# Two layers of a two-block transformer on one core: another order of steps in the first block's mixing stage

## What is computed

```
mod = silu(c) @ w_mod + b_mod;  h = rms(x, ln1) * (1 + sc1) + sh1
p = h @ w_in     # qa ka va | qi ki wi | qb kb vb | qc kc vc, heads of 64
x = x + g1 * (rms(concat(oa, ob, oc)) @ w_o)
h = rms(x, ln2) * (1 + sc2) + sh2
x = x + g2 * (silu(h @ w_gate) * (h @ w_up)) @ w_down
```

## Time and profile before

| | |
|---|---|
| median of 3 runs | 3133.84 us (3128.38 to 3138.25) |
| the profiled execution | 3130.37 us, its span 3128.6 us |
| PE busy | 2908.3 us (93%) |
| DVE busy | 1787.2 us (57%) |
| ACT busy | 756.2 us (24%) |
| POOL busy | 931.1 us (30%) |
| DMA | 313.28 MB, mean 100 GB/s |

### The profile page before, as it was taken

The page is one execution under the profiler, slowest core; times in us unless marked ns, Lnnn a source line. Parts: engine busy times, 40 slices in busy tenths (PEclk is TensorE's granted clock), DMA queues, the critical chain, the costliest instruction groups (busy, mean ns, idle before and its releaser), DMA issues.

```text
span 3128.6 us, 33693 instructions
## 1 busy us (share of the span) xinstructions
PE 2908.3 (93%) x12126; PEld 2133.1 (68%) x12126; DVE 1787.2 (57%) x3803; ACT 756.2 (24%) x1781; POOL 931.1 (30%) x794
## 2 busy tenths in 40 slices
PE   8888999999997899999989988999999998899997
PEld 4354688888544578888854456888884454688886
DVE  2673469388367447938854545877824634551433
ACT  2354310000235431000022353201112335320111
POOL 0301224443330124444412202344440400344442
PEclk9989999999998799999989988999999998899998
DMA  6115034244221013434421101254421210122221
GB/s 256 64 61 215 28 138 166 101 148 170 91 80 61 1 55 121 175 108 156 154 76 56 61 27 68 108 183 186 156 100 57 59 50 23 40 94 96 81 81 54
DMA packets 45412, 313.28 MB, mean 100 GB/s; under 512 B 5424, under 2 KB 5552, under 8 KB 31040
## 3 DMA queue, kind: packets, MB, share of 16 engines
q1 hardware_dynamic: 42912, 306.88, 27.0%
q10 hardware_dynamic: 2304, 4.20, 0.6%
q0 software_dynamic: 32, 0.07, 0.0%
HBM read 298.53 MB, written 2.10 MB: 96 GB/s over the span
## 4 chain that ended last, share of the span: by engine, by line
PE 70%; DVE 18%; ACT 6%; issue 3%; DMA 1%; POOL 1%; DVEq 0%; SPq 0%; ACTq 0%; POOLq 0%
PE bank L1114 39%; PE bank L1094 9%; PE bank L1440 7%; PE bank L1168 3%; DVE nw L2067 3%; PE bank L1264 2%; DVE sel L2304 2%; DVE m L2303 1%; PE bank L1307 1%; DVE SPT L2368 1%; ACT SPT L1756 1%; PE bank L1294 1%; PE bank L1229 1%; PE bank L1567 1%; DMA sel<-in_mod_pieces 1%
## 5 line engine op out<-in xcount | busy, mean ns | idle before, releaser
L1000 POOL TENSOR_TENSOR SPT<-ring 128x512 f32<-128x512 f32 (+2 forms) x140 | 175.2, 1252 | 956.3 <-DMA ring<-in_slabs 493.0
L1114 PE MATMUL bank<-U,ring 128*128 128x256 f32 x1728 | 412.2, 384 | 10.8 <-DVE U L2101 10.5
L1114 PEld LDWEIGHTS bank<-U,ring 128*128 128x128 f32 x1728 | 332.8, 193 | 58.4 <-DVE U L2101 12.5
L2067 DVE SCALAR_TENSOR_TENSOR nw<-sel,c,nw 128x256 f32<-128x256 f32 x504 | 321.7, 638 | 31.2 <-DMA sel<-in_mod_pieces 13.5
L1114 PE MATMUL bank<-U,SPT 128*128 128x256 f32 x1296 | 312.5, 381 | 3.0 <-POOL SPT L1005 3.0
L1114 PEld LDWEIGHTS bank<-U,SPT 128*128 128x128 f32 x1296 | 247.4, 191 | 37.7 <-POOL SPT L1005 4.4
L1114 PE MATMUL bank<-hT,SPT 128*128 128x256 f32 x1088 | 257.1, 379 | 0.0
L1440 PE MATMUL bank<-hT,ring 128*128 128x512 f32 x544 | 249.7, 607 | 7.1 <-ACT hT L1873 7.1
L2127 DVE TENSOR_TENSOR rb<-bank,nw 128x256 f32<-128x256 f32 x108 | 45.5, 422 | 355.9 <-PE bank L1114 259.1
L1114 PE MATMUL bank<-hT,ring 128*128 128x256 f32 x1088 | 246.1, 379 | 0.0
L1114 PEld LDWEIGHTS bank<-hT,ring 128*128 128x128 f32 x1088 | 207.0, 190 | 28.0 <-DMA ring<-in_slabs 0.3
(11 more groups left out here) (344 smaller groups left out, 4501.9 us busy)
## 6 DMA issues: line engine op xcount, KB each, us to landing
ring<-in_slabs SPq DMA_DIRECT2D x86, 2048.0 KB, 8.0
sel<-in_mod_pieces SPq DMA_DIRECT2D x144, 512.0 KB, 4.5
ring<-in_slabs SPq DMA_DIRECT2D x8, 1536.0 KB, 7.0
ring<-in_slabs SPq DMA_DIRECT2D x8, 1280.0 KB, 8.3
tab<-U SPq DMA_DIRECT2D x40, 128.0 KB, 2.0
U<-in_slabs SPq DMA_DIRECT2D x2, 2048.0 KB, 22.5
tmp<-nw ACTq DMA_DIRECT2D x16, 256.0 KB, 2.9
ring<-in_slabs SPq DMA_DIRECT2D x2, 1808.0 KB, 11.7
```

The lines of the kernel that those rows point to most:

```text
L1000: pool.tensor_tensor(e1, a21, a22, ALU.add).then_inc(*pool_order.up())
L1114: mm = pe.matmul(into[j][:, c:c + HALF], lhs[:, k, :], rhs[:, k, :], start=(begin and k == 0), stop=(end and k == kp - 1))
L2067: ins = dve.scalar_tensor_tensor(a, w[:, k, :], c[:, j:j + 1], a, ALU.mult, ALU.add)
```

## The change

1. The tiles are projected in the order 2, 0, 1, 10, ... instead of 0, 1, 2, 10, ... Since slabs hold four tiles in this order, the table of weights is cut by the same list.
2. The values of block 1 come first (`V_ORDER`), the rest one by one behind `idx 1`, `idx 2` and `idx 3`, each with three rounds of top-k. The weighted index sum waits only for its own block's values.
3. One weave takes the place of two: dense tiles over -0.01 to 0.48, all fourteen groups over 0.2 to 0.95, the other top-k rounds over 0 to 0.5, the stick-breaking heads over 0.5 to 0.96, the modulation products over 0.45 to 0.74 (layer 0), `wo 0` from 0.74 (layer 0) or 0.68 (layer 1) to 1.02.
4. Waits follow: the key exchange of the index tile is issued by SP one tile later, `idx` waits for the rope of tile 1, and the value consumers for the last of `V_ORDER`.

```diff
--- before.py
+++ after.py
@@ -177,12 +177,13 @@
 
 PROJ, ROWS, TURN, OUT, SMALL = (0, 1), (2, 3), (4, 5), (6,), (7,)
 QI, KI, KA, QA, QB, KB, KC, QC = 0, 2, 3, 4, 6, 8, 10, 12
-TILES1 = (0, 1, 2, 10, 12, 13, 14, 15, 4, 5, 6, 7, 8, 9)
+TILES1 = (2, 0, 1, 10, 12, 13, 14, 15, 4, 5, 6, 7, 8, 9)
+V_ORDER = (1, 2, 3, 0)
 NT1 = len(TILES1)
 ROPED = [n for n in TILES1 if n not in (6, 7, 8, 9)]
 NORMED = [n for n in ROPED if n > 1]
 SHARED = (KI, KC)
-TURNED_BEHIND = {("v", 0): ROPED[:2], ("kq", 0): ROPED[2:3], ("qa", 0): ROPED[3:6], ("qb", 0): ROPED[6:]}
+TURNED_BEHIND = {("v", 0): ROPED[:3], ("kq", 0): ROPED[3:4], ("qa", 0): ROPED[4:7], ("qb", 0): ROPED[7:]}
 PAIRED = [i // 2 + HD // 2 * (i % 2) for i in range(HD)]
 SLAB_OF_TILE = {n: (("qi", "kq", "qa", "qb")[k // 4], k % 4) for k, n in enumerate(TILES1)}
 V_A, V_WI, V_B, V_C, V_N = 0, 64, 68, 324, 452
@@ -343,36 +344,37 @@
     rounds = [[("topk", i, r)] for i in range(1, QT) for r in range(TOPK // 8)]
 
     def tile(m):
-        sums = [("pss", TILES1[m - 1])] if 0 <= m - 1 < NT1 and TILES1[m - 1] in NORMED else []
+        sums = [("pss", TILES1[m - 1])] if 0 <= m - 1 < NT1 and TILES1[m - 1] in NORMED and m != 4 else []
         rope = [("rope", TILES1[m - 2])] if 0 <= m - 2 < NT1 and TILES1[m - 2] in ROPED and m != 4 else []
         if m >= NT1:
             return [sums + rope]
         n = TILES1[m]
         return [[("pj", n, 0)], [("pj", n, 1)] + sums, [("pj", n, 2)], [("proj", n)] + rope]
 
-    for m in range(6):
-        if (l, m) == (0, 2):
+    for m in range(4):
+        if (l, m) == (0, 1):
             o.append(("tables",))
         o += [st for part in tile(m) for st in part]
-        if m == 3:
-            o += [("rope", KI)] + [("projv", i) for i in range(QT)]
-        if m >= 3:
-            o += [("idx", m - 2, hp) for hp in range(2)]
-        if m >= 4:
-            o += [st for chunk_ in rounds[:8] for st in chunk_]
-            rounds = rounds[8:]
+        if m == 2:
+            o += [("projv", V_ORDER[0])]
+    o += [("rope", TILES1[2])]
+    for i in range(1, QT):
+        o += [("idx", i, hp) for hp in range(2)] + [("projv", V_ORDER[i])]
+        o += [st for chunk_ in rounds[3 * i - 3:3 * i] for st in chunk_]
+        if i == 1:
+            o += [("pss", KC)]
+    rounds = rounds[9:] + [[("seldone", i)] for i in range(1, QT)]
     dense = []
-    for m in range(6, NT1 + 2):
+    for m in range(4, NT1 + 2):
         dense += tile(m)
-    o += woven((-0.03, 0.92, dense), (0.37, 1.01, group_slots(range(NC1))),
-               (0, 1.15, rounds + [[("seldone", i)] for i in range(1, QT)]))
     mods = []
     if l == 0:
         for s in range(MOD_FIRST, MOD_SLABS):
             mods += [[("mg", s)], [("mp", s)]]
         mods.append([("modb",)])
-    o += woven((0, 0.96, stick_slots()), (0.08, 0.95, group_slots(range(NC1, len(GROUPS1)))),
-               (0, 0.55, mods), (0.55 if l == 0 else 0.1, 1, [[("wo", 0, n)] for n in range(KT)]))
+    o += woven((-0.01, 0.48, dense), (0.2, 0.95, group_slots(range(len(GROUPS1)))), (0, 0.2, rounds[:18]),
+               (0.2, 0.5, rounds[18:]), (0.5, 0.96, stick_slots()), (0.45, 0.74, mods),
+               (0.74 if l == 0 else 0.68, 1.02, [[("wo", 0, n)] for n in range(KT)]))
     for n in range(KT):
         o += [("wo", 1, n, 0), ("xq", n, 0)] + ([("xa", n - 1, 0)] if n > 1 else [])
     o += [("S",) + FFN1[0], ("S",) + FFN1[1]]
@@ -398,7 +400,7 @@
 
 SLABS1 = ([("qi", 0), ("v", 0), ("kq", 0), ("qa", 0), ("qb", 0)]
           + [("wo", s) for s in range(2)] + ffn_slabs(1))
-LAST1 = {("qi", 0): ("proj", 10), ("v", 0): ("projv", 3), ("kq", 0): ("proj", 15), ("qa", 0): ("proj", 7),
+LAST1 = {("qi", 0): ("proj", 10), ("v", 0): ("projv", V_ORDER[-1]), ("kq", 0): ("proj", 15), ("qa", 0): ("proj", 7),
          ("qb", 0): ("proj", 9)}
 LAST1.update({("wo", 0): ("wo", 0, KT - 1), ("wo", 1): ("wo", 1, KT - 1, 1)})
 LAST1.update({slab_of(1, u): product(u, 3) for u in FFN1 if closes(u)})
@@ -948,8 +950,8 @@
                             sp.wait_ge(*s1["rope"].after(l, k - 1))
                         for e in range(2):
                             sp.dma_start(tab[e:P:2, k % 2, :], PT[1 - e:P:2, t, :]).then_inc(halves_turned[k % 2], 16)
-                        if k in (roped_at[KI], roped_at[KC] + 1):
-                            t = SHARED[k != roped_at[KI]]
+                        if k in (roped_at[KI] + 1, roped_at[KC] + 1):
+                            t = SHARED[k != roped_at[KI] + 1]
                             sp.wait_ge(*s1["rope"].after(l, roped_at[t] + 1))
                             for e in range(2):
                                 sp.dma_start(PT[HD * e:HD * e + HD, t + 1, :],
@@ -1259,7 +1261,7 @@
                         pe.wait_ge(*sl1.ready(l, key))
                         w8 = quarters(ring[:, sl1.slot(l, key), 0:WIDTHS[(1, name)]], KT)
                         for k in (2 * part, 2 * part + 1):
-                            if n == 0:
+                            if n == TILES1[0]:
                                 pe.wait_ge(*s1["h"].after(l, k + 1))
                             mm = pe.matmul(bank[b][:, :], w8[:, k, P * col:P * col + P], hT[:, k, :], start=(k == 0),
                                            stop=(k == KT - 1))
@@ -1277,7 +1279,7 @@
                                   stop=True).then_inc(*done)
                     elif kind == "idx":
                         _, i, hp = st
-                        pe.wait_ge(*s1["rope"].after(l, roped_at[KI] + 1))
+                        pe.wait_ge(*s1["rope"].after(l, roped_at[QI + 1] + 1))
                         pe.wait_ge(keys_shared[0], 32 * (l + 1))
                         for j in range(2):
                             p = slice(HD * j, HD * j + HD)
@@ -1311,7 +1313,7 @@
                     elif kind == "bpv":
                         h = st[1]
                         pe.wait_ge(*s1["ba"].after(l, h + 1))
-                        pe.wait_ge(*bk1.taken(l, ("projv", QT - 1)))
+                        pe.wait_ge(*bk1.taken(l, ("projv", V_ORDER[-1])))
                         for j in range(QT):
                             for kt in range(j + 1):
                                 c = tri[kt] + P * (j - kt)
@@ -2281,9 +2283,8 @@
                         _, i, hp = st
                         n = P * (i + 1)
                         dve.wait_ge(*s1["rl"].after(l, 2 * (i - 1) + hp + 1))
-                        if i == 1 and hp == 0:
-                            for j in range(QT):
-                                dve.wait_ge(*bk1.taken(l, ("projv", j)))
+                        if hp == 0:
+                            dve.wait_ge(*bk1.taken(l, ("projv", i)))
                         to = sel[:, i, 0:n]
                         for j in range(2):
                             r = relu[:, 2 * hp + j, 0:n]
@@ -2710,16 +2711,17 @@
 
     if blk == 1:
         w = inputs["w_in"][l]
-        if kind == "qi":
-            return tiled(heads(np.concatenate([w[:, 384:704], w[:, 256:320], w[:, 1988:2116]], axis=1)))
+        def tile_columns(n):
+            at = {0: 384, 1: 512, 2: 640, 4: 0, 5: 128, 6: 708, 7: 836, 8: 964, 9: 1092, 10: 1988,
+                  12: 1476, 13: 1604, 14: 1732, 15: 1860}[n]
+            if n == KI:
+                return heads(np.concatenate([w[:, at:at + HD], w[:, 256:320]], axis=1))
+            return heads(w[:, at:at + P]) if n in ROPED else w[:, at:at + P]
+
+        if kind in ("qi", "kq", "qa", "qb"):
+            return tiled(np.concatenate([tile_columns(n) for n in TILES1 if SLAB_OF_TILE[n][0] == kind], axis=1))
         if kind == "v":
             return cols("w_in", (320, 384), (704, 708), (1220, 1476), (2116, 2244))
-        if kind == "kq":
-            return tiled(heads(w[:, 1476:1988]))
-        if kind == "qa":
-            return tiled(np.concatenate([heads(w[:, 0:256]), w[:, 708:964]], axis=1))
-        if kind == "qb":
-            return cols("w_in", (964, 1220))
         if kind == "wo":
             return tiled(inputs["w_o"][l][512 - 512 * s:1024 - 512 * s])
         if kind == "gu":
```

## The result

The changed kernel takes 3145.32 us in the median of 5 runs (3142.30 to 3150.94), the kernel before 3130.46 us beside it (3127.40 to 3138.25, 5 runs): a ratio of 1.0044, 95% interval 1.0024 to 1.0063. It is slower by 0.4%, and the interval leaves no change out. The forecast was 3109, the range 3078 to 3138: the time lies outside, on the side of rival 1, whose figure was 3144.

What follows compares the result with a forecast made beforehand. It took 118 us of loss (PE idle or slow) in both layers' mixing stages, most beside DVE's selection, as all the change could touch. Gains of 9.9 us in layer 1 and 14.6 in layer 0, together 24.5, gave 3109; range 3078 to 3138.

Steps and rivals of the forecast that it cites:

- rival 1: Stretch without filler after the last tile runs at 1.2 GHz: layer 1 +13, layer 0 -3, total 3144; chance 0.13.
- up to the last tile: Mixing stage from its first product to the last projection tile: loss 3 us in layer 1, 4 in layer 0.
- to the first bz: Last tile to first stick-breaking scores: about 18 us in layer 1, loss 12 (bounds 5 and 18); layer 0 loss 9.
- bz to (bpv, 0): Start of stick-breaking: 41 us for 20 of PE work, loss 21 in layer 1 (bounds 14 and 31), 13 in layer 0.
- the rest: After (bpv, 0) to the stage's end: 72 us of work, loss 19 in layer 1 (bounds 12 and 25), 13 in layer 0.
- Index tile first: Start of the stage: PE reaches (idx, 1) at T = 34.4 against 54.5; first top-k round at 39 instead of 68.5.
- Selection beside projections: DVE's top-k beside the projection tiles: 14 us waiting for head sums, through at T = 160, 38 us sooner.
- PE, adding up the same prices, finishes the last tile at T = 145: End of the projections in layer 1: last tile at T = 145, us from the stage's first product.
- It keeps its length, and ACT now carries three c groups' exponentials and copies: Chain from bz to (bpv, 0): ACT carries 9.7 us more, 7 on the chain; 41 us against 34.3 before.
- At the old rate the loss is 15.7 x 72 / 67.5 = 16.7: After (bpv, 0), layer 1: loss per work unchanged, 16.7; bare closing chain of some 4.5 us makes it 19.
- The sum: Mixing stage losses together: layer 1 55 against 64.9, layer 0 39 against 53.6; 24.5 us gained.
- large gain: Groups and stick-breaking fill one another's waits, loss per work as in the old stick stage: 63 us gained, 3071; chance 0.15.

Runs made afterwards that it cites:

- wo_end96: The changed kernel with `wo 0` spread to 0.96 instead of 1.02; 3151.1 us, 1.0049 of the kernel before.
- c_behind: `wo_late` with three of eight c groups moved, in both layers, from among the tiles to the second weave; 3148.9 us, 1.0059 of the kernel before.
- new_head: The changed kernel with the two weaves of the kernel before, their start drawn forward, in place of its single weave; 3113.5 us, 0.9939 of the kernel before.
- new_weave: The kernel before, its head kept, with the change's single weave; 3168.8 us, 1.0111 of the kernel before.
- wo_late: `new_head` with layer 1's `wo 0` starting at 0.5 of the second weave instead of 0.1; 3124.9 us, 0.9974 of the kernel before.
- fill: The changed kernel plus 24 useless constant products a layer, before the waits of `br` and `bpv`; 3183.6 us, 1.0160 of the kernel before.

## Why the prediction was wrong

The sum was of losses, a stretch's length less busy time x clock. Worked out in the same way from the profiles, in us, layer 1 / layer 0:

| term | before | said | measured |
|---|---|---|---|
| up to the last tile | 25.8 / 25.7 | 3 / 4 | 16.4 / 16.8 |
| to the first bz | 8.1 / 8.0 | 12 / 9 | 4.8 / 7.7 |
| bz to (bpv, 0) | 16.2 / 11.5 | 21 / 13 | 22.9 / 21.8 |
| the rest | 15.7 / 9.4 | 19 / 13 | 23.0 / 18.7 |
| together | 65.8 / 54.6 | 55 / 39 | 67.1 / 65.0 |

By its own steps, layer 1 unless said:

- **Index tile first**: (idx, 1) at T = 36.3 (said 34.4), first round at 40.6 (39). Right.
- **Selection beside projections**: DVE waited 13.7 us for the roots of head sums (said 14). Right. But the last round came at T = 172.1, not 160: DVE was busy 106 us of the 132 between the first and the last round, as priced, and idle for 26, of which 13.7 are the waits for roots.
- **"PE, adding up the same prices, finishes the last tile at T = 145"**: the first step that failed. It ended at 164.9, with a loss of 16.4 us where the sum had 3 (16.8 for 4 in layer 0). Some loss up to the last tile was there before, and nearly all of it was taken to go away. The rows of PE up to there (busy us, mean ns of one, idle before):

```profile
L1266 PE MATMUL bank<-hT,ring 128*128 128x512 f32 x224 | 104.4, 616 | 3.2 <-ACT hT L1652 3.2
L1096 PE MATMUL bank<-ring,hT 128*128 128x452 f32 x64 | 25.2, 547 | 0.0
L1278 PE MATMUL bank<-sqb,cst 128*128 128x512 f32 x16 | 10.0, 713 | 5.3 <-ACT sqb L1672 5.3
L1341 PE MATMUL bank<-U 64*128 64x256 f32 (+1 forms) x48 | 6.5, 393 | 3.8 <-DVE U L2280 3.8
L1368 PE MATMUL bank<-VT,yB 128*128 128x64 f32 x41 | 5.1, 271 | 0.3 <-ACT yB L1769 0.3
L1287 PE MATMUL bank<-U 64*128 64x256 f32 (+2 forms) x24 | 4.7, 508 | 0.0
```

  Tiles, values, head sums and index scores are 104.4 + 25.2 + 10.0 + 4.7 = 144.3, near the 145. The groups' own products come on top (16 us: 6.5 and 5.1 above, 3.7 and 0.8 of transposes; the rows overlap one another by some 6 us), and 10.3 us of idle, most of it waits for ACT's squares and for a rope (5.3 and 3.8). The prediction doesn't list the terms of its 145. Its printed prices make 132 without the groups (fourteen tiles at 6.87, eight head sums at 0.86, the values 24.4, index scores some 5), so what it left out can't be told for sure; that it had next to no idle time and no slow clock in it can.
- **From the last tile to the first bz**: said 18 us, measured 10.8 (18.8 in layer 0).
- **"It keeps its length, and ACT now carries three c groups' exponentials and copies"**: said 41 us, in layer 1 44.6, inside its bounds. ACT was busy 24.6 us there (said 23.8). In layer 0 it was 55.4, a loss of 21.8 for 13: the modulation products and groups' steps both stand between the first bz and its running sum, 36.0 us later (220.19 to 256.19), and the clock was 0.73 where it had been 0.83. The modulation products, taken for cover, did not keep it short.
- **"At the old rate the loss is 15.7 x 72 / 67.5 = 16.7"**, with the bare closing chain 19, for the rest: the second step that failed. Busy time by clock leaves 98.9 - 87.2 x 0.87 = 23.0 (bounds 12 and 25) in layer 1 and 100.6 - 93.1 x 0.88 = 18.7 in layer 0 (said 13). The closing gaps were as said (3.39 and 3.09 us), but `wo_end96` shows that they don't decide. The rate was taken from a stage with a groups alone beside the chain, and now c groups stand there too; `c_behind` shows that this costs.
- **The sum**: I assumed that loss adds to a fixed work. The losses come to 67 and 65 us (said 55 and 39), and "work" itself came out 6 and 2 us larger than before. 12 + 26 + 8 = 46 us is the distance to the profiled execution (3150.9 against 3105.9, within a microsecond).

What failed in the whole is the claim that the loss shrinks: 118 us were to become 94, and it came out at 132. The head did save loss (33.9 us up to the first bz in layer 1 before, 21.2 now), and the single weave lost more behind it (31.9 before, 45.9 now), which `new_head` and `new_weave` show in the time, at -19 and +35 us.

**Rival 1** had the time (3144) and half of the mechanism. Its half clock is there, 0.69 between bz and (bpv, 0) in layer 1 and 0.73 in layer 0, but in layer 1 it was 0.68 before too (0.83 in layer 0). `wo_late` prices the missing filler of layer 1 at 8 to 11 us, where the rival had 23, from -10 to +13. Nor did the clock need a `wo` product to rise: in `wo_late` it is 0.50 up to 1020.22, with the running sum under way since 1017.70, and 0.96 in the 5 us behind. So that its figure was hit is in part luck. The other and larger part, groups in the queues of the stick-breaking chain, stood in none of the rivals as a loss of its own, though "large gain" counted on its opposite. It goes the other way: three groups are 11 to 13 us beside tiles and 18 or more beside the chain.

By the rule of "SBUF — State Buffer" of the Trainium skill, Who interferes with whom, the prediction had estimated up to 16 us a layer. The 16 norm steps took 19.9 us of DVE here and 17.5 before: 2.4 us more. The long rows are there and the change added little to them. "TensorE: Matmul & The Clock Gate" of the Trainium skill, What's actually happening, holds that activity releases the throttled state. The clock of `fill` agrees behind (bpv, 0) (0.95 for 0.88), not before it in layer 1 (0.65 for 0.69), and the 15.00 us of `new_head` with PE busy throughout at 0.53 do not bear it out.
